# Expert stage of a hybrid decoder step: per-token gathers against two dense passes over all experts

## The reference, cut to what matters

```python
def peer_ffn(h, wq, sub_keys, u_tab, v_tab):
    q = (x @ wq).reshape(n, PEER_HEADS, 2, PEER_KEY_DIM // 2)          # 8 heads, two halves of 64
    s = jnp.einsum('nhpk,hpek->nhpe', q, sub_keys)                     # 128 scores for each half
    s1, i1 = lax.top_k(s[:, :, 0], 16)
    s2, i2 = lax.top_k(s[:, :, 1], 16)
    cand_s = s1[..., :, None] + s2[..., None, :]                       # 256 candidates a head
    cand_i = i1[..., :, None] * 128 + i2[..., None, :]
    top_s, pick = lax.top_k(cand_s, 16)
    idx  = take(cand_i, pick)                                          # 128 experts of 16384 a token
    gate = jax.nn.softmax(top_s, axis=-1)
    act  = gelu(einsum('nd,ned->ne', x, u_tab[idx]))                   # x . u[e], exact gelu
    return einsum('ne,ned->nd', gate * act, v_tab[idx])                # sum of gate * act * v[e]
```

## Time and profile before

| | before |
|---|---|
| median of 3 runs | 6640.57 us (6621.8 to 6645.34) |
| profiled execution, its time by the page's span | 6651.1 us |
| mean granted TensorE clock of that execution | 0.62 |
| busy: PE, PEld | 2041.9 us (31%), 1122.8 us (17%) |
| busy: DVE, ACT, POOL | 4002.0 us (60%), 442.1 us (7%), 2699.0 us (41%) |
| moved by DMA | 1292.69 MB, mean 194 GB/s |

### The profile page before, as it was taken

The page is one execution under the profiler, slowest core; times in us unless marked ns, Lnnn a source line. Parts: engine busy times, 40 slices in busy tenths (PEclk is TensorE's granted clock), DMA queues, the critical chain, the costliest instruction groups (busy, mean ns, idle before and its releaser), DMA issues. The chain is left out here.

```text
span 6651.1 us, 37510 instructions
## 1 busy us (share of the span) xinstructions
PE 2041.9 (31%) x6954; PEld 1122.8 (17%) x6954; DVE 4002.0 (60%) x7053; ACT 442.1 (7%) x877; POOL 2699.0 (41%) x2674
## 2 busy tenths in 40 slices
PE   7966446760000000000079664467500000000000
PEld 2434125430000000000024331364300000000000
DVE  1222442247887977978812325422478889788787
ACT  1112011110000000000011120111100000000000
POOL 0000001006777777777600000020077777776775
PEclk8975667875555555555589766678755555555555
DMA  5101520007888988989751016101089889888897
GB/s 205 51 29 39 172 59 0 28 29 266 308 304 284 329 284 295 328 285 316 282 180 51 29 39 190 41 1 34 27 299 315 299 292 328 283 300 302 286 315 270
DMA packets 463974, 1292.69 MB, mean 194 GB/s; under 512 B 50768, under 2 KB 155289, under 8 KB 463590
## 3 DMA queue, kind: packets, MB, share of 16 engines
q0 software_dynamic: 299520, 1090.65, 47.5%
q1 hardware_dynamic: 127400, 166.42, 7.8%
q10 hardware_dynamic: 36864, 33.57, 1.6%
HBM read 1279.23 MB, written 11.44 MB: 194 GB/s over the span
## 5 line engine op out<-in xcount | busy, mean ns | idle before, releaser
L1753 DVE CUSTOM_DVE_ANT_0 arena<-arena 128x1024 f32<-128x1024 f32 x1024 | 1229.0, 1225 | 407.4 <-DMA arena<-in_peer_u_dram,arena 380.9
L1608 POOL DMA_INDIRECT arena<-in_peer_u_dram,arena x1024 | 1277.7, 1248 | 447.8 <-issue 207.7
L1773 DVE SCALAR_TENSOR_TENSOR arena<-arena 128x1024 f32<-128x1024 f32 x1024 | 1256.6, 1289 | 83.4 <-DMA arena<-in_peer_v_dram,arena 66.4
L1608 POOL DMA_INDIRECT arena<-in_peer_v_dram,arena x1024 | 1072.1, 1047 | 449.4 <-POOLq L1606 207.4
L1624 PE MATMUL bank<-arena 128*128 128x256 f32 (+1 forms) x160 | 49.4, 476 | 1995.7 <-PEq L1622 1993.1
L1630 PE MATMUL bank<-arena 8*128 8x512 f32 x8 | 7.5, 1087 | 1638.9 <-PEq L1628 1638.9
L907 POOL TENSOR_TENSOR arena<-arena 128x512 f32<-128x512 f32 x56 | 70.7, 1265 | 1039.1 <-SPq L898 794.0
L1210 POOL MEMSET arena<- 128x2048 f32 (+1 forms) x4 | 5.5, 1382 | 944.4 <-POOLq L693 944.4
L1624 PEld LDWEIGHTS bank<-arena 128*128 128x128 f32 (+1 forms) x160 | 33.8, 217 | 2010.5 <-issue 2003.3
L1605 POOL COPY arena<-arena 128x4 int32 x512 | 227.2, 444 | 343.0 <-POOLq L1604 339.9
L440 PE MATMUL bank<-arena 128*128 128x512 f32 (+5 forms) x896 | 323.3, 518 | 0.0
(11 more groups left out here) (348 smaller groups left out, 4217.0 us busy)
## 6 DMA issues: line engine op xcount, KB each, us to landing
arena<-in_w_ada_dram SPq DMA_DIRECT2D x24, 2048.0 KB, 7.9
arena<-in_cache_sb_k_dram SPq DMA_DIRECT2D x256, 128.0 KB
arena<-in_cache_sb_v_dram ACTq DMA_DIRECT2D x256, 128.0 KB, 2.9
arena<-in_w_in_dram SPq DMA_DIRECT2D x12, 2048.0 KB
arena<-in_peer_u_dram,arena POOLq DMA_INDIRECT x1040, 5.7
arena<-in_peer_v_dram,arena POOLq DMA_INDIRECT x1040, 5.9
arena<-in_w_out_dram SPq DMA_DIRECT2D x2, 4096.0 KB
arena<-in_peer_wq_dram SPq DMA_DIRECT2D x2, 4096.0 KB
```

The source lines that it names most:

```text
L1608: pool.indirect_dma_start(G_[lot * LOT + j], None, tables[which], bass.IndirectOffsetOnAxis(ap=IS[lot][:, j:j + 1], axis=0)).then_inc(gath ...
L1753: vec.tensor_tensor_reduce(G_[j], G_[j], O[:, t, :], 1.0, 0.0, ALU.mult, ALU.add, A8[:, j:j + 1]).then_inc(ring_free, 1)
L1773: vec.scalar_tensor_tensor(a, G_[j], AV[:, bass.ds(i * GR + j, 1)], a, ALU.mult, ALU.add).then_inc(dve_own, 1)
```

## The change

The indirect gathers for the prompt tokens go. In their place every expert is computed for every prompt token, in two passes, with two float32 scratch tensors in DRAM between them (`act_d`, expert x expert group x token, and `g_d`, the dense gate table in 16 blocks of 32 tokens; 32 MiB each).

First pass, 128 steps `e`, each with 128 experts: SP loads 128 rows of `peer_u` (512 KB, four buffers in `MOD9`); PE transposes them (eight 128x128 transposes), ACT copies the transposes out of PSUM (two 128x512 copies), PE multiplies them with `HT` one step later (eight matmuls of 512 columns), ACT applies gelu to the 128x512 result and SP stores two steps' results at a time. Between these, from step 16 on, the gates of the four prompt tiles are turned into dense tables, 24 steps for each tile: for each token DVE makes a one-hot matrix of the second index times the gate, POOL one of the first index, and PE multiplies the two (128x128x128), four tokens to a PSUM bank; ACT copies the bank with a stride into a staging tile and SP stores 32 tokens at a time (2 MiB). `choose(t+1)` runs on DVE in the same steps, a piece in each.

Second pass, 128 steps: SP loads the results and gates of eight steps at a time (2 MiB + 2 MiB, two buffers each), ACT's queue loads 128 rows of `peer_v` (512 KB, four buffers), DVE multiplies results by gates (128x512), and PE accumulates eight matmuls of 512 columns, one into each of the eight PSUM banks (four token tiles by two halves of the width), over all 128 steps. DVE then multiplies the banks by the modulation gate and adds them to the residual. The sample tokens keep their gathers, 8 for each table, in the second pass' shadow of DVE.

The diff, cut to its core (constants, arena layout and semaphores left out):

```diff
+                for e in range(3):
+                    sp.dma_start(UR[e], u_rows[e]).then_inc(u_landed[e], 16)
...
+            FIRST, STEPS, BANKS_T = 16, 24, P // BT4
+            turn = lambda t: FIRST + STEPS * t
+                    banks_of.setdefault(turn(t) + 2 + b * (STEPS - 2) // BANKS_T, []).append((t, b))
+            SAMPLE_AT = turn(NT) + 2
+            PREFETCH_AT = SAMPLE_AT + 8
...
                 @block.gpsimd
                 def _(pool):
...
-                    pool.sem_inc(ring_free, GR - 1)
                     for t in range(NT):
                         pool.wait_ge(dve2pool, 1).then_inc(dve2pool, -1)
-                        for which in range(2):
-                            with pool.Fori(0, SLOTS // GR) as i:
-                                for lot in range(GR // LOT):
-                                    pool.wait_ge(ring_free, LOT).then_inc(ring_free, -LOT)
-                                    nc.gpsimd.tensor_copy(IS[lot], IDI[:, t, bass.ds(i * GR + lot * LOT, LOT)]).then_inc(pool_own, 1)
-                                    pool.wait_ge(pool_own, 1).then_inc(pool_own, -1)
-                                    for j in range(LOT):
-                                        pool.indirect_dma_start(G_[lot * LOT + j], None, tables[which],
-                                                                bass.IndirectOffsetOnAxis(ap=IS[lot][:, j:j + 1], axis=0)).then_inc(gathered[lot * LOT + j], 16)
+                        for b in range(BANKS_T):
+                            if n >= RING:
+                                pool.wait_ge(oa_free, 1).then_inc(oa_free, -1)
+                            for j in range(BT4):
+                                i_ = nc.gpsimd.tensor_scalar(OA[:, at + j, :], cst("iota128"), IT[:, 1, b * BT4 + j:b * BT4 + j + 1], None, ALU.is_equal)
+                            i_.then_inc(oa_ready, 1)
...
                 @block.tensor
...
+                    def gates_bank(t, b):
+                        n = t * BANKS_T + b
+                        pe.wait_ge(ob_ready, 1).then_inc(ob_ready, -1)
+                        pe.wait_ge(oa_ready, 1).then_inc(oa_ready, -1)
+                        if b >= 2:
+                            pe.wait_ge(g_free, 1).then_inc(g_free, -1)
+                        for j in range(BT4):
+                            last = pe_.matmul(ps[6 + n % 2][:, j * P:(j + 1) * P], OA[:, at + j, :], OB[:, at + j, :], start=True, stop=True)
+                        last.then_inc(g_done, 1)
+                        if b == BANKS_T - 1:
+                            pe.wait_ge(g_free, 2).then_inc(g_free, -2)
...
+                    for e in range(P + 1):
+                        if e < P:
+                            pe.wait_ge(u_landed[e % 4], 16).then_inc(u_landed[e % 4], -16)
+                            for k in range(KD):
+                                last = pe_.transpose(ps[2 * (e % 2) + k // 4][:, (k % 4) * P:(k % 4 + 1) * P], UR[e % 4][:, k * P:(k + 1) * P], ident)
+                            last.then_inc(t_done, 1)
+                        for t in range(NT):
+                            if e == turn(t) + 1:
+                                one_hots(t)
+                        for t, b in banks_of.get(e, ()):
+                            gates_bank(t, b)
+                        if e == SAMPLE_AT:
+                            sample_rows()
+                        if e >= 1:
+                            f = e - 1
+                            pe.wait_ge(ut_ready, 1).then_inc(ut_ready, -1)
+                            for k in range(KD):
+                                last = pe_.matmul(ps[4 + f % 2][:, :], UT[:, f % 2, k, :], HT[:, k, 0:SEQ], start=(k == 0), stop=(k == KD - 1))
+                    pe.wait_ge(s_free, 1).then_inc(s_free, -1)
+                    pe.wait_ge(dve2pe, 1).then_inc(dve2pe, -1)
+                    for e in range(P):
+                        pe.wait_ge(v_landed[e % 4], 16).then_inc(v_landed[e % 4], -16)
+                        pe.wait_ge(w_ready, 1).then_inc(w_ready, -1)
+                        wt = ACH[(e // CH) % 2][:, e % CH, :]
+                        for t in range(NT):
+                            for half in range(2):
+                                last = pe_.matmul(ps[2 * t + half][:, :], wt[:, t * P:(t + 1) * P], VR[e % 4][:, half * GBLK:(half + 1) * GBLK],
+                                                  start=(e == 0), stop=(e == P - 1))
...
                 @block.scalar
...
+                    for e in range(P + 2):
+                        act.wait_ge(t_done, 1).then_inc(t_done, -1)
+                        if e < P:
+                            act.sem_inc(u_free, 1)
+                        if e >= 2:
+                            gelu(e - 2)
+                        if e < P:
+                            act_.copy(UT[:, e % 2, 0:4, :], ps[2 * (e % 2)][:, :].rearrange("p (k n) -> p k n", k=4))
+                            act_.copy(UT[:, e % 2, 4:8, :], ps[2 * (e % 2) + 1][:, :].rearrange("p (k n) -> p k n", k=4)).then_inc(ut_ready, 1)
+                        for t in range(TILES):
+                            if e == turn(t):
+                                gate_exp(t)
+                        for t, b in banks_of.get(e, ()):
+                            act_.copy(stage.rearrange("p e n -> p n e"), ps[6 + n % 2][:, :].rearrange("p (n e) -> p n e", n=BT4)).then_inc(act_own, 1)
...
+                    for e in range(P - 4):
+                        act.wait_ge(v_free, 1).then_inc(v_free, -1)
+                        act.dma_start(VR[e % 4], v_rows[e + 4]).then_inc(v_landed[e % 4], 16)
...
                 @block.vector
...
+                            for j in range(BT4):
+                                i_ = vec.tensor_scalar(OB[:, at + j, :], cst("iota128"), IT[:, 0, b * BT4 + j:b * BT4 + j + 1],
+                                                       IT[:, 2, b * BT4 + j:b * BT4 + j + 1], ALU.is_equal, ALU.mult)
...
+                        wt = ACH[c][:, e % CH, :].rearrange("p (g n) -> p g n", n=SPAN)
+                        vec.tensor_tensor(wt, wt, GCH[c][:, :, e % CH, :], ALU.mult).then_inc(w_ready, 1)
...
+                    for n in range(8):
+                        dve.wait_ge(pe2dve, 1).then_inc(pe2dve, -1)
+                        vec.tensor_tensor(TX[n], ps[n][:, :], GP[:, c], ALU.mult).then_inc(dve_own, 1)
+                        vec.tensor_tensor(X[:, t, c], X[:, t, c], TX[n], ALU.add)
```

More of the change, by code:

```diff
@@ L1634, in _ @@
[L1634 to L1635 removed]
+                        last = pe_.matmul(ps[4 + i][0:NB, :], cst("gather8"), ACC[:, i * GBLK:(i + 1) * GBLK], start=True, stop=True)
                     last.then_inc(pe2dve, 1)
```

369 lines of the change are left out of this document (246 added, 123 removed).

## The result

| | before | after |
|---|---|---|
| median of 4 runs | 6642.95 us | 6958.69 us |
| lowest to highest | 6621.80 to 6662.80 | 6950.52 to 6961.69 |
| profiled execution, span | 6651.1 us | 6957.6 us |
| mean granted clock | 0.621 | 0.902 |

The changed kernel takes 1.0479 times as long (95% interval 1.0448 to 1.0510).

The account below looks back on a forecast made before the run. Old expert block bound by DVE at 1889 us a layer; new one by PE: 20 + 1157 + 2 + 889.5 + 13 = 2082 us, 386 more in two layers, so 7027 us; 8 in 10 for 6940 to 7260.

Parts of the forecast that it names:

- The matmuls: Both passes on PE: 2048 float32 matmuls of 512 columns a layer at 0.869 us each, 1779 us.
- The transposes: First pass on PE: 1024 a layer at 0.138 us each, 141 us, with ends of 113 and 225.
- The last-bank waits: First pass, last gate bank of each tile: PE waits for ACT about 2 us, four times, 8 us.
- the sample rows: First pass, step 114: two replicating matmuls on PE and a wait for two DVE copies, about 4 us.
- Edges: Expert block outside the passes' streams: start 20 us, hand-over between passes 2 us, end 13 us a layer.
- the narrower range: Whole kernel, between the ends of the unknown costs of transposes, gates and waits: 6955 to 7310 us.
- The wider range: Whole kernel, the range of 8 in 10: 6940 to 7260 us.
- the rule for no change: Whole kernel within 0.5%, 6607 to 6674 us, said to need a layer under 1901 us; chance 2%.
- The clock: Both passes taken at granted clock 1.00; rival: it falls in the first pass, 7.6 to 9.3 ms, chance 4%.
- The transfers: Rival in the second pass: strided loads bind below 151 GB/s, +142 to +440 us a layer; chance 6%.
- The helper engine: Rival in the first pass: POOL's one-hots above 1.6 us or small-bank stalls, +50 to +300 us a layer; chance 8%.
- The vanishing small products: Rival in the first pass: transposes and gate products, 254 us a layer, hide behind large matmuls, kernel 6520 us; chance 2%.

Follow-up runs that it names:

- experiment 3: Changed kernel with POOL writing each of its one-hots three times, waiting for each extra one to end; 7698.34 us.
- experiment 5: Changed kernel without the second pass's matmuls of the upper half of the width except in the last step, all transfers kept; 6104.18 us.
- experiment 8: Kernel with three bfloat16 products reduced to high x high only, no low halves made; 4975.18 us, 0.748 times the kernel before.
- experiments 3 and 4: Changed kernel with POOL writing each one-hot three times, 7698.34 us, and, in the second of the two, twice, 7004.23 us.
- experiment 2: Changed kernel with one gate product of each four kept on PE, one-hots, copies and stores unchanged; 6794.06 us.

## Why the prediction was right

**The bound of before**, 1889 us a layer, and the reading that the rest of the kernel stays put: right, to 1 us over 2874.

**The matmuls.** 0.434 us a record was read from the start of one group to the start of the next; measured 0.4293 in a long stream (1024 matmuls in 879.15 us, 0.859 each). The group used is 6.95 us long where the stream needs 6.87 for as many; the 0.08 at the group's ends was multiplied by 128 steps. 10 us a pass too much, and the range gave this term no spread.

**The transposes.** 0.138 us each against 0.109, 29 us a layer too much and the largest miss. The group of eight in the earlier trace rows that I divided wasn't an unbroken stream. PE's weight loads of the kernel before at that place show it:

```profile
1264.52 0.42 PEld L1447 LDWEIGHTS bank<-arena 128*128 128x128 f32 x4 [0.45 <-issue]
1265.14 0.42 PEld L1447 LDWEIGHTS bank<-arena 128*128 128x128 f32 x4 [0.20 <-issue]
```

The loads of eight transposes come as four and four with 0.20 us between them. Taking the hole for part of the pace gave 0.138; the lower end that I had put beside it, half of the half-clock 0.22, was the truth.

**The gate products**: 113 forecast, 113.9 measured. **The last-bank waits**: 8 forecast, 12.5, **the sample rows** 4 forecast, 7.3: the waits were about right (9.1 and 4.7), what I left out is that the clock can fall right behind them. **Edges**: start 20 forecast and 20.1 measured, hand-over 2 and 1.4, end 13 and 12.5.

**The sum.** Per layer -29 (transposes), -20 (matmuls, two passes), +1, +4.5, +3.3, -0.6, -0.5 give -41; measured 2041.5 against 2082, -40.5. Twice that takes 7037 to 6956, and the profiled execution has 6957.6. No term is left over. But this is at the edge of the narrower range: its lower end allowed 36 us a layer, less than the 40.5 found. That the median is still 4 us above that end (6955) is luck: before's profiled execution was taken as 10.5 us above its median, the changed kernel's is 1.1 us below its own. The wider range, from 6940, holds without it. In the rule for no change, a layer under 1901 should read 1906: half of 6674 less 7027, added to 2082.

**The clock** stayed at 0.99 to 1.00 in both passes, with transposes in the first one at 112 of 1128 us. The reason given, that PE is never idle for more than some 2 us, was too weak: behind three waits in each layer, of 1.6, 2.20 and 2.49 us, the clock did fall, and that costs 6.1 us a layer. By the Trainium skill ("TensorE: Matmul & The Clock Gate", Part 4: PE-mode transpose) transposes don't count as PE work for the clock. The trace gives that rule no effect here: between streams of ordinary matmuls a run of eight transposes costs 0.87 us and the clock stays up; the three falls stand behind waits. In experiment 3 part of the rival's mechanism, a lower clock in the first pass, does appear; what differs there is PE's waits, and not the transposes.

**The rivals.** The clock: refuted for this kernel but for 6 us a layer, and seen at size once PE is made to wait. The transfers: refuted, with a factor of two to spare (experiment 5), and likely the bound once PE needs some 260 us for the pass, which then takes 394 (experiment 8). The helper engine: costs nothing here; its price once it binds is higher than I took (experiments 3 and 4). The vanishing small products: refuted, for the gate products by experiment 2 and for the transposes by the timeline.

**In a sentence**: the change trades 1243 us of DVE's row work and 220 us of gather waits a layer for 1758 us of float32 matmuls and some 225 us of transposes and gate products on PE, and PE does nothing else. With 3 bfloat16 products for each float32 one the same plan is the faster one.

## What to carry to other kernels

When a change turns a sparse stage into a dense one on PE, the count of matmul records times the pace of an unbroken stream decides it; read that pace from a long run of the same shape and type, start to start, and look into the group for holes before dividing. Where it then loses by less than a tenth, ask for the operand type before the schedule: moving every wait gave 31 us, splitting the operands 677, at the price of the low bits that three products leave out. A short wait of PE costs its own length and, where the clock falls behind it, more: a third on average here.

## What the runs showed of the hardware

POOL and DVE held each other up in two pairs of operations that read on-chip memory. DVE's 128x512 product of two operands took 2.64 us instead of 0.69 beside a POOL subtraction of 2.13 us; with that subtraction gone from POOL it was 0.69 again. POOL's one-hot of 0.60 us took 2.74 beside DVE's 128x2048 product of 2.28 us. By the Trainium skill ("SBUF — State Buffer", Who interferes with whom) a DVE instruction with two inputs in that memory and a GpSimd instruction that reads it exclude each other for a whole instruction, and the one that is first goes first. The first half agrees with both cases. The second agrees with the product, which started 0.04 us behind and was the long one; it doesn't with the one-hot, which is shown as starting 0.08 us ahead of DVE and was the long one too, though starts of POOL are rough.

A pause of PE of 1.6 to 2.5 us inside a stream at granted clock 1.00 can drop the clock to its lower level for a few us: windows of eight matmuls right behind such pauses show 0.80 and 0.73 and last 8.64 and 9.47 us instead of 6.87. It needn't: of the four waits at last banks in a layer two, of 2.20 us each, left it at 1.00 (6.94 us), and the other two, of 2.20 and 2.49, didn't. Where PE waited at 51 of a layer's 128 banks (experiment 3), the work itself took 198.5 us more over both layers, on 549.6 us of waits.
